# Requesting x by ScalarE's progress, zero matmuls in early gaps, and the last chunk in one piece per column

## What is computed

```python
u = rmsnorm(x, g_mix)
proj = u @ w_in                      # 1024 -> 9216, nine blocks of 1024
a_b, a_c, a_h, a_z, b_v, b_g, b_z, gate_a, gate_b = split(proj)
s = a_c * a_h
ya = (a_b * dwconv3(s) * silu(a_z)) @ w_out_a
v = b_v * sigmoid(b_g)               # stage 2 of the kernel
c = dwconv31(concat(history, v)) + b_conv_b
yb = (silu(layernorm(c)) * silu(b_z)) @ w_out_b
h = x + (sigmoid(gate_a) * ya + sigmoid(gate_b) * yb) @ w_o
h = h + sigmoid(rmsnorm(h) @ w_pg) * (p @ w_pe)
y = rmsnorm(h)
```

## Time and profile before

| | us |
|---|---|
| median of 3 runs | 902.71 (901.27 to 1062.96) |
| the profiled execution | 902.14 |
| its span, first to last instruction, slowest core (core 2) | 900.6 |
| spans of the eight cores | 894.3 to 900.6 |
| PE busy | 847.8 (94%) |
| DVE busy | 507.9 (56%) |
| ACT busy | 301.5 (33%) |
| POOL busy | 147.9 (16%) |

### The profile page before, as it was taken

How to read it: one execution, slowest core, us unless ns; L and a number is a source line. 1 busy time by engine, 2 the same in 40 slices (tenths; PEclk the granted TensorE clock), 3 DMA queues, 4 the chain that set the end, 5 groups by cost and what they waited for, 6 DMA issues and landing times.

```text
span 900.6 us, 15270 instructions; the slowest of 8 cores (894.3 to 900.6 us)
## 1 busy us (share of the span) xinstructions
PE 847.8 (94%) x4922; PEld 449.7 (50%) x5000; DVE 507.9 (56%) x794; ACT 301.5 (33%) x566; POOL 147.9 (16%) x275
## 2 busy tenths in 40 slices
PE   4799699998999999999999999999999999999993
PEld 4798355554445445454545444444444444444441
DVE  1456134555798777777777753332333234787775
ACT  3674134344424333323332321111111111444442
POOL 3231211110101010110101011100001001344441
PEclk9999899999999999999999999999999999999997
DMA  9781999997312030312302085234320325766642
GB/s 180 237 172 36 171 160 174 175 131 123 64 34 47 1 59 13 59 21 40 60 12 49 12 176 94 41 54 71 48 47 4 50 60 114 216 171 179 169 131 95
DMA packets 94110, 84.41 MB, mean 94 GB/s; under 512 B 53552, under 2 KB 74928, under 8 KB 93488
## 3 DMA queue, kind: packets, MB, share of 16 engines
q0 software_dynamic: 27920, 31.20, 24.7%
q1 hardware_dynamic: 66112, 52.22, 23.9%
HBM read 86.80 MB, written 15.61 MB: 114 GB/s over the span
## 4 chain that ended last, share of the span: by engine, by line
PE 84%; DMA 7%; DVE 3%; issue 2%; SPq 1%; ACT 1%; POOL 1%; DVEq 0%; POOLq 0%; ACTq 0%
PE ps L409 65%; PE ps L822 6%; PE ps L843 6%; PE ps L577 4%; DMA t_v<-vd 3%; DMA t_ring<-w_in 2%; PE ps L849 1%; SPq L346 1%; DMA t_x<-x 1%; DMA t_v<-t_vrow 1%; PE ps L645 1%; PE ps L479 1%; DMA vd<-t_vrow 1%; DVE t_uT L482 1%; DVE t_accs L616 0%
## 5 line engine op out<-in xcount | busy, mean ns | idle before, releaser
L409 PE MATMUL ps<-t_uT,t_ring 128*128 128x512 bf16 (+2 forms) x3208 | 541.6, 327 | 12.9 <-DVE t_uT L482 5.9
L409 PEld LDWEIGHTS ps<-t_uT,t_ring 128*128 128x128 bf16 x3264 | 287.8, 99 | 255.8 <-issue 13.3
L796 DVE TENSOR_TENSOR t_tmp<-ps,t_tmp 128x512 f32<-128x512 f32 (+1 forms) x80 | 48.7, 610 | 151.5 <-PE ps L409 150.7
L343 POOL DMA_DIRECT2D t_ring<-w_in x72 | 38.7, 540 | 395.1 <-PE ps L409 383.2
L793 ACT ACTIVATE t_tmp<-ps 128x512 f32<-128x512 f32 (+1 forms) x80 | 42.4, 532 | 177.1 <-PE ps L409 177.0
L754 ACT ACTIVATE t_tmp<-t_tmp,t_vecs 128x512 f32<-128x512 f32 (+1 forms) x40 | 30.0, 749 | 122.0 <-DVE t_tmp L751 122.0
L513 DVE TENSOR_TENSOR t_vrow<-ps,t_tmp 128x256 bf16<-128x256 f32 (+2 forms) x56 | 25.6, 461 | 75.5 <-PE ps L409 60.3
L409 PE MATMUL ps<-t_cb,t_ring 128*128 128x512 bf16 (+1 forms) x320 | 65.4, 347 | 0.0
L409 PE MATMUL ps<-t_yaT,t_ring 128*128 128x512 bf16 (+1 forms) x312 | 64.9, 346 | 0.4
L577 PE MATMUL ps<-t_v,t_Wp 128*128 128x336 bf16 x320 | 51.7, 321 | 11.0 <-DMA t_v<-vd 6.6
L822 PE MATMUL ps<-t_wo_t,t_cb 128*128 128x512 bf16 x264 | 60.9, 379 | 0.4
(11 more groups left out here) (96 smaller groups left out, 745.4 us busy)
## 6 DMA issues: line engine op xcount, KB each, us to landing
t_ring<-w_in POOLq DMA_DIRECT2D x72, 256.0 KB, 6.7
t_x<-x SPq DMA_DIRECT2D x17, 512.0 KB, 5.7
t_xs<-x SPq DMA_DIRECT2D x17, 512.0 KB, 4.3
t_cb<-t_c SPq DMA_DIRECT2D x64, 128.0 KB, 5.9
y<-t_yt SPq DMA_DIRECT2D x16, 512.0 KB, 3.2
vd<-t_vrow SPq DMA_DIRECT2D x28, 128.0 KB, 5.0
t_v<-vd SPq DMA_DIRECT2D x7, 512.0 KB, 9.2
t_ring<-w_oa POOLq DMA_DIRECT2D x8, 256.0 KB, 7.1
```

Of the source, the lines that this page charges most:

```text
L343: S.add("pool", lambda e: e.dma_start(out=out, in_=in_), reads=reads, writes=list(writes) + [swq()], dma=key)
L409: S.add("pe", lambda e, k=k: e.matmul(ps[:, b, 0:n], lhsT=ring[k_ring][:, k, :], rhs=rhs_fn(k), start=(k == 0), stop=(k == NCH - 1)), read ...
L796: S.add("dve", lambda e, p=p, t=t: e.tensor_tensor(out=tmp[t][:, 0:n], in0=ps[:, p, 0:n], in1=tmp[t][:, 0:n], op=ALU.mult), reads=[f"ps{p} ...
```

## The change

**Loads.** Tiles 2 to 5 of x are no longer requested when ring tiles have landed but by ACT's and POOL's progress: tile 2 when tile 0 is squared, tile 3 when tile 1 is, tile 4 when tile 1's scale is there, tile 5 when tile 2 is squared. Later tiles follow in order (before, tile 6 was requested ahead of tile 3). The identity comes with vecs in one load of 96 KB and DVE casts it to bf16; the 32 KB load on POOL's queue is gone. Weights are requested four first, two after tile 0's scale, two after tile 1's.

**PE's early work.** `busy(n)` multiplies n times a buffer of zeros (128x512) into a free bank whose content nobody reads: 16 before the first transposes, 10 and twice 4 behind transposes. The first three tiles are copied, transposed and multiplied in two halves, with separate resources, so that the first four matmuls of a group can start on the first half.

**Order.** `FIRST` is longer: it covers all of chunk 0 and the transposes up to tile 6, and column 3 comes last. Chunk 1 and 2 stay in pieces of 256, with three steps of stage 1 in some; chunk 3 is one piece of 512 per column. `conv_load(0)` and `(1)` stand behind columns 1 and 2 of that piece, and the two histories are requested in the first piece of chunk 2. The stores of the samples' v, the mask and the conv weights are requested after the first piece instead of the third.

```diff
+        S.add("dve", lambda e: e.memset(xb1[3][:], 0.0), writes=["xb13", "xb1h3"])
+        S.add("dve", lambda e: e.tensor_copy(out=idb[:], in_=onesf), reads=["onesf"], writes=["idb"])
         s1_load(1)
-        pump(4)
-        s1_load(2, ["ring1"])
+        def busy(n):
+            b = balloc()
+            for _ in range(n):
+                S.add("pe", lambda e: e.matmul(ps[:, b, :], lhsT=xb1[3][:, 0:128], rhs=xb1[3][:, 0:512], start=True, stop=True),
+                      reads=["xb13"], writes=[f"ps{b}"])
+            bfree(b)
+        busy(16)
...
+        def parts(i):
+            return [(0, 512), (512, 512)] if i < 3 else [(0, D)]
...
+        def hist_load(j):
+            s = j % 2
+            pdma(v8[s][:, :, 260:340], h8_d[j], [], [f"v8{s}h"], f"v8{s}h")
+
         def conv_load(j):
             s = j % 2
-            pdma(v8[s][:, :, 260:340], h8_d[j], [], [f"v8{s}h"], f"v8{s}h")
+            if j >= 2:
+                hist_load(j)
...
         s1_a1(0)
+        s1_load(2, ["ssq0"])
+        pump(2)
         s1_a2(0)
-        pump(2)
-        s1_load(3, ["ring3"])
-        s1_load(4, ["ring5"])
-        s1_load(5, ["ring5"])
         s1_b(0)
-        nxt = [1]
-        s1_a1(1)
+        busy(10)
+        nxt = [7]
...
+        s1_a1(1)
+        s1_load(3, ["ssq1"])
+        s1_load(4, ["rsd1"])
+        pump(2)
         s1_a2(1)
+        FIRST = [(0, 0), (s1_b, 1), (busy, 4), (s1_a1, 2), (s1_load5, None), (0, 1), (s1_a2, 2), (1, 0), (1, 1), (s1_b, 2),
...
-        PIECES = [(0, 256, 128, (0, 1, 0, 0)), (0, 384, 128, (1, 0, 1, 0))]
-        PIECES += [(c, o, 256, (1, 0, 1, 0)) for c in (1, 2, 3) for o in (0, 256)]
+
+        PIECES = []
+        PIECES += [(1, 0, 256, (1, 0, 1, 0)), (1, 256, 256, (1, 1, 1, 0)), (2, 0, 256, (1, 1, 0, 1)),
+                   (2, 256, 256, (1, 0, 1, 0)), (3, 0, 512, (0, 0, 0, 0))]
...
                 if si == 2 and o == 0 and j < 2:
+                    hist_load(j)
                     vs_load(j)
-                if si == 3 and o > 0 and 1 <= j < 3:
+                if si == 3 and 1 <= j < 3:
                     conv_load(j - 1)
```

More of the change, by code:

```diff
@@ L467, in s1_a2 @@
             rs_ap, rs_res = s1st[i]
[L468 to L471, removed]
+            for c, w in parts(i):
+                S.add("act", lambda e, c=c, w=w: e.activation(out=xb1[bq][:, c:c + w], in_=xs1[xq][:, c:c + w], func=AF.Copy,
+                                                              scale=rs_ap),
+                      reads=[f"x1{xq}", rs_res], writes=[f"xb1{bq}" if c == 0 else f"xb1h{bq}"])
+            while NXS <= xnext[0] <= i + NXS and xnext[0] < len(TILES):
+                s1_load(xnext[0])
         def s1_b(i):
@@ L476, in s1_b @@
             bq = i % NXB
[L477 to L484, removed]
-                reads=[f"ps{b}", "vecs"], writes=[f"uT{t}"])
-            bfree(b)
+            for c, w in parts(i):
+                b = balloc()
+                k0, nk = c // 128, w // 128
+                for k in range(nk):
+                    S.add("pe", lambda e, k=k, k0=k0, b=b: e.transpose(
+                        out=psb[:, b, k * 128:(k + 1) * 128], in_=xb1[bq][:, (k0 + k) * 128:(k0 + k + 1) * 128],
+                        identity=idb[:]),
+                        reads=[f"xb1{bq}" if c == 0 else f"xb1h{bq}", "idb"] + ([f"xb1h{bq}"] if w == D else []),
+                        writes=[f"ps{b}"])
+                S.add("dve", lambda e, k0=k0, nk=nk, b=b: e.tensor_tensor(
+                    out=uT[si][:, k0:k0 + nk, o:o + 128],
+                    in0=psb[:, b, 0:nk * 128].rearrange("p (k t) -> p k t", t=128),
+                    in1=vecs[:, V_GMIX + k0:V_GMIX + k0 + nk].unsqueeze(2).to_broadcast([128, nk, 128]), op=ALU.mult),
+                    reads=[f"ps{b}", "vecs"], writes=[f"uT{t}" if c == 0 else f"uTh{t}"])
+                bfree(b)
         vst_ctr = [0]
@@ L1211 @@
     shared = dict(w_in=cols(w_in[0]), w_oa=cols(w_out_a[0]), w_ob=cols(w_out_b[0]), w_o=rows(w_o[0]),
-                  w_pg=rows(w_pg[0]), w_pe=rows(w_pe[0]), tw=tw, mask=mask, vecs=vecs, gfin=gfin, gple=gple, ident=ident)
+                  w_pg=rows(w_pg[0]), w_pe=rows(w_pe[0]), tw=tw, mask=mask, vecs=vecs, gfin=gfin, gple=gple)
     def phases(a):
```

43 lines of the change are left out of this document (23 added, 20 removed).

## The result

The changed kernel takes 891.35 us (median of 4 runs, 889.12 to 892.19) beside 901.99 for the kernel before on the same chip. The ratio is 0.9886, with a 95% interval of 0.9855 to 0.9917: a gain that is there, and under 2%. The profiled execution took 892.19 us; the forecast was 889.8, the range 881.0 to 896.5. Where the page of before named core 2 as the slowest, that of after names core 6, with a span of 890.4 us.

What follows compares the result with a forecast made beforehand. PE, busy 847.8 of 900.6 us, was taken as the bound, so only its lost time could be won back. 3.3 us early plus 9.0 at the handover made 12.3 off 902.14: 889.8 us, range 881 to 896.5.

Steps and rivals of the forecast that it cites:

- Sum and sign: Whole kernel: 3.3 us from the early stage plus 9.0 at the handover, 12.3 us faster, 889.8 us.
- Head, 3.3 us: PE's work up to the end of the four columns: ends at 89.6 us instead of 92.9.
- The tile chain: Early stage: ACT squares, POOL scale, ACT copy, one tile after another, 3.3 to 3.7 us per tile, bound PE.
- Weights of column 4, 1.72 us: Handover to the convolution: ring slots free 10.4 us before the stage ends, so PE's 1.72 us wait goes.
- The v wait, 5.23 us: Handover: v load takes 9 to 12 us, there before 12.3 us are up, so PE's 5.23 us wait goes.
- the text's own signs of being wrong: Ring-tile waits past 26 us, low clock over 7 us, v load over 12.3 us, or growing waits from 107 to 260.
- Rival (c): Handover: v wait stays because four columns' slots refill beside the load; handover worth 5.2 us, total 893.6; chance 0.10.
- The clock, 2.07 us: Convolution start: without a pause the first 20 matmuls take 3.02 us instead of 5.09.
- (a): Early x requests are served behind queued weights, so only the handover to the convolution pays: 893.1 us; chance 0.14.
- (b): Early stage gains its full 12.8 us, PE having enough loaded work from 18 us on: 880.3 us; chance 0.06.
- (d): Zeros and short waits leave PE at 1.2 GHz; 906.3 us if down from 11 to 50 us; chance 0.04.
- (e): Start of the kernel: PE's start was never the limit, so the zeros bring nothing; no separate chance given.

Runs made afterwards that it cites:

- the head alone: The changed kernel with the last chunk in two pieces again and the histories back in conv_load; ratio to the kernel before 0.9941.

## Why the prediction was right, point by point

**Sum and sign.** 12.3 us were forecast from the profiled execution of before; its counterpart after gained 9.95 (902.14 to 892.19), the ratio makes it 10.3, and the mean of the eight cores' spans 12.0. The sum was right for a typical core; the 2.4 us between forecast and profile are in the slowest one. That it came out so well on the mean is partly luck. Two misses cancel: head and weights gave 7.0 us where 5.0 were forecast, the v wait and the clock 5.5 where 7.3 were.

**Head, 3.3 us.** Stage 1's last matmul of the four columns comes at about 88.7 on core 6 (*ready* there, 96.55, less the 7.8 us of column 4's three jobs), against 89.6 forecast and 92.9 before. *Ready* on the mean gained 7.0 where head and weights together were to give 3.3+1.72 = 5.0; the head alone moved it by 5.7. The tile chain was as forecast: tiles 4, 5 and 6 at 28.84, 32.49, 36.52 for 28.7, 32.4, 36.2. Some 1.4 us of the surplus were there before the change: the sum was made on core 2, which was *ready* at 102.16, and the mean of the eight was 103.57. The rest is in two places: on core 6 the waits in the pieces are 0.61+0.47+0.26 = 1.3 us, not 2.1, and there PE never waits for weights early on, where I had a pause until 18 us for weight 3 (the second to fourth unit are done by 19.0, as the row at 16.38 has it). Six of the other cores do wait for weights before 25 us, by 0.59 to 1.83 in all.

**Weights of column 4, 1.72 us.** Gone, as forecast; with the head alone changed they are still there (0.81 to 2.18 us by core).

**The v wait, 5.23 us: the step that failed inside a sum that held.** The text took 9 to 12 us for the v load and its request about 4.5 us before the stage's end. On core 6 the last store took 6.82, not 5.09, so the request came at 86.29, 2.4 before the end; the load then took 12.99. 79.41+0.06+6.82+12.99 is 99.28, and PE was there at 96.55: 3.12 us of wait with the start of the matmul, where none was forecast. A load of over 12.3 us was one of the text's own signs of being wrong, and it came on two cores (12.99 on core 6, 12.94 on core 3). Rival (c) named the reason, that four columns' slots refill beside this load; I gave it 0.10. Its 893.6 is nearer to the profiled 892.19 than the forecast (1.4 against 2.4 off), and farther from the median (2.2 against 1.6): it was half true, its wait there and its head too small. On the mean 1.13 us of wait are left, so most cores were nearer to the forecast. With weights held back the load takes 4.5 us and the wait is zero: what the step needed was the load's company, not its size.

**The clock, 2.07 us.** It followed the wait: 1.84 us on the mean, 0.40 (5.09 to 4.69) on the slowest core, because that one waited.

**The rivals.** (a) falls: the head pays, 0.59% alone and 5.7 us of *ready*. (b) falls: in the early stretch ACT's copies start 3.65 to 4.01 us apart; taking squares first in the later steps gives 1.7 us of *ready*, not 9.5. (d) falls by the time; of its low clock there were some 3 us on three cores (0.50 from 16 to 18), and none on core 6. (e) holds for the zeros, worth 0.15 us of *ready* and nothing in the time, which the sum had as well.

**The step missing from the sum.** It was made on one core and taken for the metric. The core that is slowest is so by its own waits: before, core 2 had not only 5.23 us at the handover but 3.20 at column 7, where core 6 of the same execution had 1.77, and its next 40 matmuls took 7.55 us, core 6's 5.87 (timeline of PE before, core 2):

```profile
213.66 7.55 PE L577 MATMUL ps<-t_v,t_Wp 128*128 128x336 bf16 x40 [3.20 <-DVE t_v L553]
```

After the change another core draws the long wait. The prediction also took matmuls of 128 columns at 58 and 117 ns, from durations that include the end of the last one; in the traces they start 56 and 107 ns apart, which moves the sum by little. A sum for the slowest core has to be made for the mean, and the spread put on top.
